# A trunk layer of attention, convolution and 32 experts: rearranged first projections, a bias table in reversed order, a later second gather and a mask by replacement

## The reference

```
h = rmsnorm(x);  [q_a k_a v_a | B C u | q_x | gate logits] = h @ w_in
y_att  = softmax(q_a k_a^T / 8 + rel_bias[bucket(i - j)]) v_a      8 heads x 64, causal, one block of 256
y_conv = B * causal_conv3(C * u)                                    512 channels
y_xatt = softmax(q_x k^T / sqrt(128)) v                             4 heads x 128
         with k, v = rmsnorm(mem) @ w_mem_kv
x = x + (sum_i sigmoid(g_i + b_i) * (y_i @ w_br_i)) @ w_out
logits = rmsnorm(x) @ w_router + b_router;  top 4 of 32, softmax over those 4
x = x + sum over the 4 of weight * (((clip(lin)+1) * g * sigmoid(1.702 g)) @ w_down + b_down)
        with [g | lin] = rmsnorm(x) @ w_gu[e] + b_gu[e], clipped at 7
out = rmsnorm(x)
```

## Time and profile before

| | |
|---|---|
| median of the runs | 1212.86 us |
| profiled execution | 1211.5 us, span 1209.6 us |
| TensorE busy | 1113.4 us (92%), 6085 instructions |
| VectorE busy | 390.0 us (32%) |
| ScalarE busy | 267.9 us (22%) |
| DMA | 452.13 MB, mean 374 GB/s, queue of SyncE 90.2% |
| chain that ended last | TensorE 51%, DMA 43%, VectorE 4% |

### The profile page before, as it was taken

One profiled execution on the slowest core, in us unless ns is written; L12 is line 12 of the kernel. 1 busy time (PEld: TensorE's weight loads), 2 busy tenths in 40 slices (PEclk: granted clock), 3 DMA queues, 4 the chain that ended last, 5 costly groups with the idle time before them and its releaser, 6 DMA issues.

```text
span 1209.6 us, 14738 instructions
## 1 busy us (share of the span) xinstructions
PE 1113.4 (92%) x6085; PEld 588.4 (49%) x6085; DVE 390.0 (32%) x656; ACT 267.9 (22%) x406; POOL 4.5 (0%) x10
## 2 busy tenths in 40 slices
PE   6999999999999998888989898888989899998996
PEld 6999899995343333333333333333333333333332
DVE  6657655573232222222222222222222222222223
ACT  5334575443011111111111111111111111111112
POOL 0000000000000000000000000000000000000000
PEclk8999999999999999999999999999999999999999
DMA  7994444668999999999999999999999999999994
GB/s 260 347 313 141 137 159 142 242 248 351 403 430 430 429 430 433 430 433 428 428 431 432 431 432 430 427 429 430 430 431 431 433 411 430 430 432 433 423 426 181
DMA packets 58230, 452.13 MB, mean 374 GB/s; under 512 B 3234, under 2 KB 34327, under 8 KB 40151
## 3 DMA queue, kind: packets, MB, share of 16 engines
q1 hardware_dynamic: 57376, 449.79, 90.2%
q0 software_dynamic: 560, 1.74, 0.4%
q10 hardware_dynamic: 263, 0.15, 0.0%
HBM read 450.60 MB, written 1.06 MB: 373 GB/s over the span
## 4 chain that ended last, share of the span: by engine, by line
PE 51%; DMA 43%; DVE 4%; issue 1%; SPq 0%; ACT 0%; DVEq 0%; ACTq 0%
DMA dring<-in_w_down_dram 37%; PE bank L1059 19%; PE bank L1377 13%; PE bank L1337 13%; DMA ring<-in_w_gu_dram 6%; DVE region_r L1010 1%; DVE region_r L1007 1%; DVE region_r L1003 1%; PE bank L1359 1%; DVE region_r L1004 1%; PE bank L1280 1%; PE bank L1251 1%; PE bank L1126 0%; PE bank L1066 0%; PE bank L1106 0%
## 5 line engine op out<-in xcount | busy, mean ns | idle before, releaser
L1337 PE MATMUL bank<-ring,region_x 128*64 128x512 f32 x2048 | 450.8, 598 | 7.9 <-DMA ring<-in_w_gu_dram 7.9
L1337 PEld LDWEIGHTS bank<-ring,region_x 128*64 128x64 f32 x2048 | 144.6, 138 | 293.8 <-issue 281.5
L1377 PE MATMUL bank<-dring,region_r 128*64 128x512 f32 x1024 | 237.7, 614 | 46.2 <-DMA dring<-in_w_down_dram 45.3
L1377 PEld LDWEIGHTS bank<-dring,region_r 128*64 128x64 f32 x1024 | 72.3, 140 | 197.4 <-issue 129.5
L1003 DVE TENSOR_SCALAR region_r<-bank 128x512 f32<-128x512 f32 x32 | 22.1, 692 | 369.2 <-PE bank L1337 369.2
L1021 DVE SCALAR_TENSOR_TENSOR y_parts<-bank,region_r,y_parts 64x512 fp32r<-64x512 f32 x32 | 23.8, 744 | 325.5 <-ACT y_parts L627 325.5
L618 ACT ACTIVATE region_r<-region_r 128x512 f32<-128x512 f32 x32 | 20.1, 629 | 429.1 <-DVE region_r L1003 429.1
L1059 PE MATMUL bank<-hT_high,w_high 128*128 128x256 f32 x384 | 110.8, 289 | 0.0
L1059 PE MATMUL bank<-hT_low,w_high 128*128 128x256 f32 x384 | 108.6, 283 | 0.0
L1059 PE MATMUL bank<-hT_high,w_low 128*128 128x256 f32 x384 | 108.6, 283 | 0.0
L692 DVE TENSOR_TENSOR w_low<-ring,w_high 128x2048 fp32r<-128x2048 f32 x39 | 89.3, 2290 | 56.9 <-ACT w_high L474 56.9
(11 more groups left out here) (234 smaller groups left out, 912.4 us busy)
## 6 DMA issues: line engine op xcount, KB each, us to landing
ring<-in_w_gu_dram SPq DMA_DIRECT2D x56, 4096.0 KB, 27.6
dring<-in_w_down_dram SPq DMA_DIRECT2D x60, 2048.0 KB, 24.3
ring<-in_w_gu_dram SPq DMA_DIRECT2D x15, 2048.0 KB, 9.6
ring<-in_w_in_dram SPq DMA_DIRECT2D x26, 1024.0 KB, 10.9
dring<-in_w_down_dram SPq DMA_DIRECT2D x8, 1024.0 KB, 16.5
ring<-in_w_mem_kv_dram SPq DMA_DIRECT2D x4, 1024.0 KB, 12.8
ring<-in_w_out_dram SPq DMA_DIRECT2D x4, 1024.0 KB, 4.8
ring<-in_w_br_conv_dram SPq DMA_DIRECT2D x2, 1024.0 KB, 7.0
```

The source lines that it names most:

```text
L1337: last = mm(ps[64 * half:64 * half + 64, :], xg[u // 2][:, c, 64 * (u % 2):64 * (u % 2) + 64], ring[:, slot0 + c, k * F + half * 512:k * F ...
L1377: last = mm(y_ps[64 * half:64 * half + 64, :], lhsT, dring[:, c // 2, at:at + 512], start=(c == 0), stop=(c == KC - 1))
```

## The change

- `PROJ` starts with the memory's values (j = 2, 3), then its keys. The pieces 1 and 2 are loaded ahead of x (x was ahead of piece 1), piece 0 in two halves with semaphores of their own, the identity is loaded by SyncE ahead of all instead of by ScalarE.
- The squares of the memory rows are summed by VectorE instead of ScalarE. TensorE does 7 products of ones before its first wait and 4 more behind the memory's transposes. Projection 0 is a function of its own, whose matmuls go by halves of the weight and of the activation, each behind its own wait. The row of norm factors and x's transposes come after projection 2 instead of after 0 and 1; the high part of piece 3 (the fourth) is taken before x is normalised.
- `hot` is built for increasing distance and `bias` is a reversed view; the flips, their copies, the flip matrix and SyncE's wait for the bias go. The table product moves behind projection 0.
- In the routing all transposes of x2 stand behind the last w_out piece; the square sum of t = 0 comes before the copies. One start sum is done before the counting, one behind it, one behind the first gather, one in expert 0. The second gather is done in expert 0 after its third chunk, the transposes of the weights after its last. The mask is made by `match_replace` of the four largest and a comparison with the logits.
- The first four experts are peeled off TensorE's loop. The first four slots of expert 2's up weights are loaded one by one, down 1 slot by slot, expert 3's up two slots at a time.

```diff
-PROJ = ([("w_mem_kv", 256 * j) for j in range(4)]
+PROJ = ([("w_mem_kv", 256 * j) for j in (2, 3, 0, 1)]
-        dist = 2 * P - 1 - i
+        dist = i - (P - 1)
-    bias = region_r[:, 0:2048].rearrange("p (h k) -> p h k", h=ATT_H)
+    bias = region_r[:, 0:2048].rearrange("p (h k) -> p h k", h=ATT_H)[:, :, ::-1]
# SyncE
+        sp.dma_start(consts[:, 0:P], a["consts"][:, 0:P]).then_inc(ident_in, 16)
         for t in range(TT):
             sp.dma_start(mem_nat[:, t, :], ...).then_inc(mem_in[t], 16)
+        for t, landed in enumerate((first_half_in, piece_in[mixer_slot(0)])):
+            sp.dma_start(first[:, 4 * t:4 * t + 4, :], first_src[:, 4 * t:4 * t + 4, :]).then_inc(landed, 16)
-            if p == 1:
+            if p == 3:
                 ... x, consts
-            if p == 4:
-                sp.wait_ge(bias_in, 16)
...
-        for c in range(2):
+        for c in range(4):
             sp.wait_ge(pieces_used, N_MIX + c + 1)
             up_chunks(2, 8 + c, c, 1)
-        for m in range(1, KC // 2):
+        for m in range(2, KC // 2):
             sp.wait_ge(pieces_used, N_MIX + 2 * m + 2)
             up_chunks(2, 8 + 2 * m, 2 * m, 2)
-        expert_down(1, 1)
-        expert_up(3, 0, N_MIX - RING + 25)
+        expert_down(1, 1, 1)
+        expert_up(3, 0, N_MIX - RING + 25, 2)
# ScalarE, start
+        act_high_part(0, memT, memT_high)
+        act_high_part(1, memT, memT_high)
+        act.wait_ge(first_half_in, 16)
+        w_high_half_part(0, w_high_half)
+        act_high_part(2, memT, memT_high)
+        act.wait_ge(piece_in[mixer_slot(0)], 16)
+        w_high_half_part(1, w_high_ready)
+        act_high_part(3, memT, memT_high)
+        w_high_part(1)
+        w_high_part(2)
         root(0)
+        ... square sums of x
+        w_high_part(3)
         root(1)
# VectorE, start
+        first_gain(0)
+        first_gain(1)
+        act_low_part(0, ...), act_low_part(1, ...)
+        first_gain(2)
+        w_low_half_part(0, w_high_half, w_low_half)
+        first_gain(3)
+        w_low_half_part(1, w_high_ready, w_low_ready)
+        act_low_part(2, ...), act_low_part(3, ...)
+        for t in range(TT):
+            if t == 1:
+                w_low_part(1)
+            dve.wait_ge(mem_in[t], 16)
+            link(dve.scalar_tensor_tensor(region_r[:, 0:1024], mem_nat[:, t, :], 1.0, mem_nat[:, t, :], ALU.mult, ALU.mult,
+                                          accum_out=norm[:, 0, t:t + 1]))
         rstd(0)
+        projection(0)
+        w_low_part(2)
+        ... diagonals, rstd(1), copy of the table of distances
# VectorE, mask
-        dve.max_index(...) x2, is_equal with the expert numbers, tensor_reduce
+        link(dve.memset(best[:, :, TOPK:], -3.4e38))
+        dve.match_replace(others[:, 0, :], best[:, 0, :], logit[:, 0, :], -3.4e38)
+        link(dve.match_replace(others[:, 1, :], best[:, 1, :], logit[:, 1, :], -3.4e38))
+        dve.tensor_tensor(mask[:, :, :], others, logit, ALU.not_equal).then_inc(mask_sb, 1)
# TensorE
+        pe.wait_ge(ones_ready, 1)
+        for _ in range(7):
+            mm(bank[3][:, 0:P], all_ones, all_ones, start=True, stop=True)
+        def first_projection():
+            for k in range(2):
+                for half in range(2):
+                    cs = range(4 * half, 4 * half + 4)
+                    if k == 0:
+                        pe.wait_ge((w_high_half, w_high_ready)[half], 1)
+                    pe.wait_ge(act_high, 2 * k + half + 1)
+                    ... high x high of the four chunks
+                    pe.wait_ge(hT_parts, 2 * k + half + 1)
+                    ... low x high
+                    if k == 0:
+                        pe.wait_ge((w_low_half, w_low_ready)[half], 1)
+                    ... high x low
-            if p in (3, 4):
-                ... the flips
-                if j == 3 and n == 5:
-                    ... transposes of x2, t = 0
+        pe.wait_ge(merged_sb, 12)
+        pe.wait_ge(gates_sb, 12)
+        for u in range(4):
+            pe.wait_ge(x2_sb, u + 1)
+            transposed(x2, u, bank[(6, 7, 0, 1)[u]], x2T_done)
+                    if first_four and u == 0 and c == 2:
+                        pe.wait_ge(passes_ready, 1)
+                        gather(y_ps, 1)
+                if first_four and u == 0:
+                    rest_of_first()
+        four_experts(0, True, False)
+        more = pe.value_load(more_i32[0:1, 0:1], min_val=0, max_val=PASSES - 1)
+        with pe.Fori(1, more * (E // 4) + (E // 4 - 1)) as i:
+            four_experts(i, False, False)
```

More of the change, by code:

```diff
@@ L594, in _ @@
                 .then_inc(x2T_copied, 1)
[L595 to L598, removed]
+        act.wait_ge(x2_sb, 4)
+        act.wait_ge(sq_done, TT + 1)
+        square_sums(x2, squares2, 2, 1)
         root(2)
@@ L693, in w_low_part, with first_gain, w_low_half_part @@
                 .then_inc(w_low_ready, 1)
-        dve.wait_ge(cols_sb, 1)
-        for u in range(4):
+        def first_gain(u):
             dve.wait_ge(hT_done, u + 1)
             with_gain(bank[4 + u], g_mem, memT, u % 2, u // 2, gained)
[L699 to L702, removed]
+        def w_low_half_part(half, high, low):
             cut = slice(half * 1024, half * 1024 + 1024)
@@ L1074, in _ @@
             transposed(mem_nat, u, bank[4 + u], hT_done)
-        pe.wait_ge(table_in, 16)
-        mm(bank[3][0:ATT_H, 0:TOEP], table, hot, start=True, stop=True).then_inc(dist_done, 1)
+            if u == 3:
+                for _ in range(4):
+                    mm(bank[3][:, 0:P], all_ones, all_ones, start=True, stop=True)
+        def first_projection():
+            high, low = [w.rearrange("p (c n) -> p c n", c=KC) for w in (w_high[0][:, :], w_low[mixer_slot(0)][:, :])]
+            for k in range(2):
+                dst, cut = bank[0][:, k * 256:k * 256 + 256], slice(k * P, k * P + P)
+                for half in range(2):
[3 more added lines that the diff above has]
+                    pe.wait_ge(act_high, 2 * k + half + 1)
+                    for c in cs:
+                        mm(dst, memT_high[:, c, cut], high[:, c, :], start=(c == 0), stop=False)
+                    pe.wait_ge(hT_parts, 2 * k + half + 1)
+                    for c in cs:
+                        mm(dst, memT_low[:, c, cut], high[:, c, :], start=False, stop=False)
+                    if k == 0:
+                        pe.wait_ge((w_low_half, w_low_ready)[half], 1)
+                    for c in cs:
+                        last = mm(dst, memT_high[:, c, cut], low[:, c, :], start=False, stop=(c == KC - 1))
+            last.then_inc(pieces_used, 1)
         def projection(u):
@@ L1154, in heads @@
                 values(j - 3)
-        pe.wait_ge(hT_parts, 4)
+        first_projection()
+        pe.wait_ge(table_in, 16)
+        mm(bank[3][0:ATT_H, 0:TOEP], table, hot, start=True, stop=True).then_inc(dist_done, 1)
         for p in range(N_PROJ):
@@ L1280, in bias_rows, with start_sum @@
             mm((gate_ps, lin_ps)[k][:, :], sel[:, :], b_parts[:, k * 512:k * 512 + 512], start=True, stop=False)
-        for t in range(TT):
-            for half in range(2):
-                mm(acc[t][half][:, :], ident, x2[:, t, half * 512:half * 512 + 512], start=True, stop=False)
+        def start_sum(t, half):
+            mm(acc[t][half][:, :], ident, x2[:, t, half * 512:half * 512 + 512], start=True, stop=False)
         pe.wait_ge(sel_ready, 1)
         bias_rows(1)
+        start_sum(0, 0)
         pe.wait_ge(counting_ready, 1)
@@ L1308, in _, with rest_of_first, four_experts @@
         gather(tr_ps, 0)
-        pe.wait_ge(passes_ready, 1)
-        gather(y_ps, 1)
-        more = pe.value_load(more_i32[0:1, 0:1], min_val=0, max_val=PASSES - 1)
-        pe.wait_ge(xg_sb, 1)
-        pe.wait_ge(weights_sb, 1)
-        for t in range(TT):
-            last = transpose(tr_ps[0:E, t * P:(t + 1) * P], wexp[:, t, 0:E], ident)
-        last.then_inc(wexpT_done, 1)
-        def four_experts(i, last_four):
+        start_sum(1, 0)
+        def rest_of_first():
+            start_sum(1, 1)
+            pe.wait_ge(weights_sb, 1)
+            for t in range(TT):
+                last = transpose(tr_ps[0:E, t * P:(t + 1) * P], wexp[:, t, 0:E], ident)
+            last.then_inc(wexpT_done, 1)
+        def four_experts(i, first_four, last_four):
             for u in range(4):
```

146 lines of the change are left out of this document (53 added, 93 removed).

## The result

The changed kernel takes 1204.77 us (median, 1204.05 to 1205.91) against 1212.55 for the kernel before, run beside it: ratio 0.994, interval [0.9928, 0.9953]. That is 7.8 us less where 10.9 less was forecast (1202.0). It is inside the range 1198 to 1207.5, which was wide enough to hold the failure of a whole term.

The account below looks back on a forecast made before the run. Expert-weight transfers were taken to fix the end once the DMA queue is full. Terms 3.44 (flips) + 2.75 (clock) + 2.2 (early start) + 2.5 (routing) = 10.9 us less, giving a median of 1202.0, range 1198 to 1207.5.

Parts of the forecast that it names:

- The bound: Expert phase: once the DMA queue is full, the end is fixed by when it becomes full; mixer microseconds come off the end.
- A, flips: Mixer, around projections 3 and 4: the 8 flip matmul passes go, reversed reads cost nothing; 3.44 us less.
- B, clock: Mixer start: at full clock projection 0 takes 5.74 us instead of 8.49; 2.75 us less.
- C, the early start: Mixer start: projection 1 at 17.2, projection 4 at about 36.7; 2.9 us less new stalls included, 0.7 taken off, 2.2 in the sum.
- D, first half: Routing up to the first expert matmul: the gather waits for h2, and that matmul comes at 291.0 instead of 293.54.
- D, second half: Expert 0: moved gather, start sum and wexp transposes make downs 0.5 us late, hidden; routing's sum over all 2.5 us less.
- two rivals together: Upper end of the range: Rival 1 and Rival 3 both happening, 1206.9 us.
- Rival 3: Routing: the queue gains nothing because the idle time turns up again between expert 0's slots; 1204.5 us, chance 0.10.
- Rival 1: Mixer start: the clock stays low in projection 0 or falls again in its waits; 1204.4 us, chance 0.13.
- Rival 4: Mixer's first head: the bias, issued later, lands too late; slower than before if after 89 us, 1216 at 92; chance 0.03.

Follow-up runs that it names:

- e4: Changed kernel with one more 2-element sigmoid on ScalarE ahead of its wait for the transposed expert weights; 1203.89 us.
- e9: e4 with all four start sums of x2 in the routing's two gaps, two ahead of the counting and two between counting and first gather; 1201.84 us.
- e10: e9 with the second gather directly behind the first, ahead of expert 0; 1201.96 us.
- e12: e10 with the loads of expert 2, down 1 and expert 3 in the coarser sizes of before; 1203.09 us.
- e5: Kernel before with the bias alone changed: increasing distance, reversed read, no flips, no SyncE wait for the bias; 1209.01 us, ratio 0.9978.
- e3: Changed kernel without the 11 products of ones; 1205.73 us.
- e7: Changed kernel with the constants loaded behind piece 8 and the root of x's norm ahead of piece 3's high part; 1203.89 us.
- e1: Mixer of the changed kernel, with routing, experts and their loads as in the kernel before; 1204.67 us, ratio 0.9938.

## Why the prediction was right, and where not

- **The bound** was read rightly. In the changed kernel the lead at 85 MB is the lead at the end to within 0.5 us, over 850 us of expert phase, and so in e4, e9 and e10. It is not exact: e12 lost 1.1 us on the way and e5 1.3.
- **A, flips, 3.44.** e5 shows 3.1 to 3.7 us of lead after the mixer and reversed reads as fast as plain ones; in time it was 2.6 to 2.8.
- **B, clock, 2.75.** Full clock through projection 0 as forecast. e3 corrects the reason: the products of ones are needed for it, yet only about 0.5 of the 2 us that they save there reach the end of the mixer. B and C together should have been priced as one chain. (The start at 29.73 that term C cites is not in the earlier trace rows.)
- **C, the early start.** Projection 1 was to start at 17.2 and does so at 17.32; projection 4 at 37.72 instead of 36.7. Piece 3 was in at 22.8 (issued 10.42, 12.4 before), not 21.5, and the nine traces under e7 show that its arrival sets projection 4. I had taken 0.7 off for stalls of VectorE; the mixer came out at 8.0 for 8.4.
- **D, first half.** Mixer and routing together: first expert matmul 10.7 us sooner, forecast 10.9. The gather waits for h2 and the mask is off the path, as forecast.
- **D, second half, is the step that failed:** "TensorE finishes its up matmuls at 306.9 against 307.45 and is 0.5 late for its downs. That is hidden: TensorE is ahead of the transfers until 420." With the mixer's 8.0 us taken off, expert 0's up matmuls end 0.6 sooner than before (298.81), as forecast, but its downs start 1.4 later (305.56), not 0.5, and it is not hidden. Between first up and first down matmul the changed kernel needs 22.8 us, the one before 18.6: 2.0 for the gather, about 1.2 for the last start sum and the wexp transposes, and the 1.2 us of ScalarE's table load, which I did not look for behind the wait that the change moved. Until about 330 the transfers live from the slots that TensorE frees, so time lost there comes back at the end: e4 takes back 0.9, the sums in the gaps 2.0 more, e9 together 2.9 with no overlap of the ranges. The term of 2.5 measured about 0 in e1. I had also priced the stage by its gaps alone. They shrank a little (busy share 0.94 for 0.92), but the engines moved less all the same (348 GB/s for 370), and no term stood for that.
- **What was luck.** The forecast missed by 2.8 us, 2.5 of it this one term. The time was inside the range because the range reached down to two rivals together, not because the routing did what was said.
- **The rivals.** Rival 3, that the queue gains nothing from the routing, is what happened: it put the time at 1204.5. Its mechanism was half right: the time was lost at expert 0's slots, but through late downs and a lower rate as well, and little of it as idle time. Rival 1's low clock came true, but at the first gather and at the last wait instead of in projection 0. Rival 4 did not occur: the read of the bias was issued at 31.30 and had landed 10.1 us later, at 41.4, before 45 and long before the first head.

## What to carry to other kernels

When work is moved off a critical chain into the stage behind it, list what each engine has queued behind every wait that moves with it; a table load of 1.28 us behind a moved copy cost more than the copy. A queue that is fed by freed slots is bound by the transfers only once it is full: until then the consumer's order is the critical path, so fill the waits of the stage before with independent work. Here that also went with a full clock in four of four profiled executions.

## What the hardware showed

- The granted clock fell in the waits of the routing in three of seven profiled executions with the start sums spread, and in none of four with the gaps filled; so few executions suggest the link but do not prove it. It fell also at the last long wait (near 1142 us, 1151 before) in six of twelve profiled executions: the changed kernel, e1, e3, e9, e10 and e12, where 32 matmuls took 8.6 to 8.8 us for 7.11. Each of these six profiled executions is above its kernel's median, by 0.3 to 1.3 us. That fits the spread of 1 to 2 us between runs of one kernel; since the other runs have no profile, it is not shown that it is all of it.
- Transposes were followed by matmuls at the high level (the passes at 9.89 of the earlier trace rows), but in e3 sixteen transposes within 3.7 us were followed by 4.4 us of matmuls at the low level, and what differs is not known. The record of the granted clock stands at 1.00 in that stretch; at the start of a kernel the spacing of the matmuls was the surer sign.
- A reversed free-dimension read of fp32 on VectorE cost nothing (0.42 us for 256 columns either way).
